# A two-block transformer forward pass on one core: the first pass over the experts as straight-line code, no token gather behind the last pair of experts, and the last expert's result leaving in two column halves

## What is computed

```
def moe_swiglu(u, w_router, w_gate, w_up, w_down):
    B, S, D = u.shape
    t = u.reshape(B * S, D)
    logits = (t @ w_router).astype(F32)
    top_vals, top_idx = lax.top_k(logits, TOP_K)
    top_w = jax.nn.softmax(top_vals, axis=-1)
    gates = jnp.sum(jax.nn.one_hot(top_idx, N_EXPERTS, dtype=F32) * top_w[..., None], axis=1)
    out = jnp.zeros((B * S, D), F32)
    for e in range(N_EXPERTS):
        y = swiglu(t, w_gate[e], w_up[e], w_down[e]).astype(F32)
        out = out + gates[:, e:e + 1] * y
    return out.reshape(B, S, D).astype(u.dtype)
```

## Time and profile before

| | |
|---|---|
| median of 3 runs | 1900.12 us (1899.29 to 1902.54) |
| the profiled execution's own time | 1900.97 us |
| its span, first to last instruction | 1899.1 us |
| time outside the span | 1.87 us |
| PE busy | 1819.6 us (96%) |
| DVE busy | 1482.6 us (78%) |
| ACT busy | 1246.3 us (66%) |
| POOL busy | 23.5 us (1%) |
| the chain that ended last | PE 85%, DVE 7%, ACT 6%, issue 2% |
| mean granted clock of PE | 0.979 |

### The profile page before, as it was taken

The page is one execution under the profiler, slowest core; times in us unless marked ns, Lnnn a source line. Parts: engine busy times, 40 slices in busy tenths (PEclk is TensorE's granted clock), DMA queues, the critical chain, the costliest instruction groups (busy, mean ns, idle before and its releaser), DMA issues.

```text
span 1899.1 us, 26739 instructions
## 1 busy us (share of the span) xinstructions
PE 1819.6 (96%) x9912; PEld 1560.7 (82%) x9912; DVE 1482.6 (78%) x1503; ACT 1246.3 (66%) x1288; POOL 23.5 (1%) x24
## 2 busy tenths in 40 slices
PE   7888999998999999999899999999999999999997
PEld 7777899887789988877788888888888888788886
DVE  7975788566567755665888988889878888798896
ACT  6966656365654435654677777777777777777776
POOL 0000000000000000000000000000000000000000
PEclk9999999999899999999899999999999999999999
DMA  9422455542235454434599999999999999999995
GB/s 373 150 89 89 156 179 186 193 175 89 89 120 190 180 185 160 165 111 152 200 384 358 394 374 338 379 364 392 373 331 373 367 396 373 331 366 377 378 371 190
DMA packets 69523, 495.69 MB, mean 261 GB/s; under 512 B 7840, under 2 KB 8224, under 8 KB 10144
## 3 DMA queue, kind: packets, MB, share of 16 engines
q1 hardware_dynamic: 67680, 487.48, 67.5%
q0 software_dynamic: 1728, 6.55, 1.6%
HBM read 488.76 MB, written 5.24 MB: 260 GB/s over the span
## 4 chain that ended last, share of the span: by engine, by line
PE 85%; DVE 7%; ACT 6%; issue 2%; DMA 0%; SPq 0%; POOL 0%; ACTq 0%; DVEq 0%; POOLq 0%
PE ps L424 26%; PE ps L426 20%; PE ps L433 20%; PE ps L435 6%; PE ps L428 6%; DVE wl L2130 2%; ACT wh L1401 2%; PE ps L1326 1%; PE ps L444 1%; PE ps L1247 1%; PE ps L839 1%; PE ps L840 1%; PE ps L844 1%; DVE hTl L2188 1%; ACT hTh L1439 0%
## 5 line engine op out<-in xcount | busy, mean ns | idle before, releaser
L3088 DVE TENSOR_TENSOR wl<-raw,wh 128x2048 fp32r<-128x2048 f32 x336 | 762.5, 2290 | 100.4 <-ACT wh L2038 99.5
L2038 ACT ACTIVATE wh<-raw 128x2048 fp32r<-128x2048 f32 x336 | 643.4, 1919 | 179.9 <-PE ps L433 179.9
L424 PE MATMUL ps<-wh,hTh 128*128 128x512 f32 (+2 forms) x1128 | 445.2, 396 | 9.5 <-issue 4.7
L426 PE MATMUL ps<-wh,hTl 128*128 128x512 f32 (+2 forms) x1128 | 436.5, 388 | 0.0
L2130 DVE TENSOR_TENSOR wl<-raw,wh 128x2048 fp32r<-128x2048 f32 x124 | 283.5, 2290 | 124.0 <-ACT wh L1401 123.8
L1401 ACT ACTIVATE wh<-raw 128x2048 fp32r<-128x2048 f32 x125 | 238.6, 1914 | 137.8 <-PE ps L433 70.2
L433 PE MATMUL ps<-wl,hTh 128*128 128x512 f32 (+2 forms) x1128 | 301.6, 387 | 0.0
L424 PEld LDWEIGHTS ps<-wh,hTh 128*128 128x128 f32 x1128 | 213.0, 189 | 54.2 <-issue 9.5
L424 PE MATMUL ps<-wh,work_r 128*128 128x512 f32 x648 | 255.7, 395 | 0.0
L426 PE MATMUL ps<-wh,work_r 128*128 128x512 f32 x648 | 253.0, 390 | 0.0
L426 PEld LDWEIGHTS ps<-wh,hTl 128*128 128x128 f32 x1128 | 213.3, 189 | 40.4
(11 more groups left out here) (432 smaller groups left out, 1539.3 us busy)
## 6 DMA issues: line engine op xcount, KB each, us to landing
raw<-in_units SPq DMA_DIRECT2D x461, 1024.0 KB, 7.0
x<-in_x SPq DMA_DIRECT2D x2, 512.0 KB, 5.3
work<-in_lru_w SPq DMA_DIRECT2D x1, 1024.0 KB, 15.0
xn<-in_mem SPq DMA_DIRECT2D x1, 1024.0 KB, 17.4
out<-x POOLq DMA_DIRECT2D x2, 512.0 KB, 6.9
consts<-in_consts POOLq DMA_DIRECT2D x1, 768.0 KB, 4.7
xn<-in_moe_gain POOLq DMA_DIRECT2D x1, 512.0 KB, 5.9
consts<-in_consts SPq DMA_DIRECT2D x1, 354.0 KB, 11.3
```

The lines of the kernel that those rows point to most:

```text
L424: nc.tensor.matmul(out, sh, mh, start=(first and j == 0), stop=False)
L426: nc.tensor.matmul(out, sl, mh, start=False, stop=False)
L2038: A(wh[:, n % SPLIT, :], raw[:, n % RAW, :], ACT.Copy).then_inc(sem("hi_made"), 1)
L3088: V.tensor_tensor(wl[:, n % SPLIT, :], raw[:, n % RAW, :], wh[:, n % SPLIT, :].bitcast(F32), ALU.subtract).then_inc(sem("lo_made"), 1)
```

## The change

PE, ACT and DVE get their first pass over the experts as straight-line code: a Python loop over eight experts in place of the hardware loop, with constants in place of the registers. The loop stays for the pass under the `If`. In the last expert of the first pass the gather, `choose`, the splitting of the gathered tokens and the preparation of three further units fall away; they stand at the beginning of the `If`'s body now, and SyncE's loads of the three units as well. The last two down units of the last expert are computed one output half after the other: half h=0 over both units, then half h=1 over both. ACT scales each half as it is done, and POOL issues one indirect DMA for each. For that, out is also seen as rows of 512 columns, and the slots' table carries three row numbers (the full row, and twice it and twice it plus one), so that a tiny matmul is four columns wide in place of two.

```
         def experts(first, last):
-            with nc.tensor.Fori(first // 2, last // 2) as p:
-                for i in range(2):
-                    expert(p, i)
+        def experts():
+            for e in range(NE):
+                expert(e // 2, e % 2, last=(e == NE - 1))
...
-            if i == 1:
+            if i == 1 and not last:
                 pe.wait_ge(sem("chosen"), p + 2)
                 pe.wait_ge(sem("bank7_free"), p * 6 + 6)
                 for q in range(4):
                     gather(q)
             pe.wait_ge(sem("expert_hid"), of(ECH, ECH))
+            if last:
+                w = {}
+                for h in range(2):
+                    hs = slice(h * HALF, (h + 1) * HALF)
+                    for half in range(2):
+                        if h == 0:
+                            w[half] = unit_of(("down", ECH - 1, half))
+                        ins = split_product(ps[:, 4 + h, :],
+                                            [(ehh[(ECH - 1) % 2][:, 2 * half + k, :], ehl[(ECH - 1) % 2][:, 2 * half + k, :],
+                                              w[half][0][:, k, hs], w[half][1][:, k, hs]) for k in range(2)],
+                                            first=False, last=(half == 1), rest=rest_of(("down", ECH - 1, half)))
+                        if h == 1:
+                            ins.then_inc(sem("unit_used"), 1)
+                        elif half == 1:
+                            ins.then_inc(sem("first_half"), 1)
+                return
...
             def hi(j):
+                if last and j >= E_UNITS:
+                    return
...
                     for h in range(2):
+                        if last and h == 0:
+                            act.wait_ge(sem("first_half"), 1)
+                        else:
+                            act.wait_ge(sem("unit_used"), of(E_UNITS, E_UNITS + SPLIT))
...
+        rows_turned(NE - 1, TT + NE - 1)
+        for h in range(2):
+            pool.wait_ge(sem("y_scaled"), 2 * NE + h + 1)
+            G_.indirect_dma_start(out_halves, bass.IndirectOffsetOnAxis(ap=out_row[:, 1 + h:2 + h], axis=0),
+                                  y[:, h * HALF:(h + 1) * HALF], None, compute_op=ALU.add).then_inc(sem("out_written"), 16)
+        pool.wait_ge(sem("out_written"), 16 * (TT + NE + 1))
```

More of the change, by code:

```diff
@@ L1249, in gather, with over_experts, expert @@
             ins.then_inc(sem("bank7_full"), 1)
-        def experts(first, last):
-            with nc.tensor.Fori(first // 2, last // 2) as p:
+        def experts():
+            for e in range(NE):
+                expert(e // 2, e % 2, last=(e == NE - 1))
+        def over_experts():
+            with nc.tensor.Fori(NE // 2, NE) as p:
                 for i in range(2):
                     expert(p, i)
-        def expert(p, i):
+        def expert(p, i, last=False):
             def of(m, n):
@@ L1333, in _ @@
             gather(q)
-        experts(0, NE)
+        experts()
         with nc.tensor.If(nc.tensor.value_load(over[0:1, 0:1], min_val=0, max_val=1)):
-            experts(NE, 2 * NE)
+            pe.wait_ge(sem("chosen"), NE // 2 + 1)
+            pe.wait_ge(sem("bank7_free"), NE // 2 * 6)
+            for q in range(4):
+                gather(q)
+            over_experts()
     @block.sync
@@ L1373, in follow @@
             load(None, n, units_d[source])
-        for j in range(SPLIT):
-            follow(N_UNITS + j, N_FIXED + j)
         sp_.wait_ge(sem("routed"), 1)
         with nc.sync.If(nc.sync.value_load(over[0:1, 0:1], min_val=0, max_val=1)):
+            for j in range(SPLIT):
+                follow(N_UNITS + j, N_FIXED + j)
             groups = (NE * E_UNITS - SPLIT) // RAW
@@ L2023, in tokens_high, with experts, over_experts, expert @@
               ACT.Copy).then_inc(sem("tokens_hi"), 1)
-        def experts(first, last):
-            with nc.scalar.Fori(first // 2, last // 2) as p:
+        def experts():
+            for e in range(NE):
+                expert(e // 2, e % 2, last=(e == NE - 1))
+        def over_experts():
+            with nc.scalar.Fori(NE // 2, NE) as p:
                 for i in range(2):
                     expert(p, i)
-        def expert(p, i):
+        def expert(p, i, last=False):
             def of(m, n):
@@ L2069, in _ @@
             tokens_high(q, q + 1)
-        experts(0, NE)
+        experts()
         with nc.scalar.If(nc.scalar.value_load(over[0:1, 0:1], min_val=0, max_val=1)):
-            experts(NE, 2 * NE)
+            for r in range(4):
+                tokens_high(r, NE // 2 * 6 + 1 + r)
+            for n in range(N_UNITS, N_UNITS + SPLIT):
+                act.wait_ge(raw_loaded[n % RAW], 16 * (n // RAW + 1))
+                act.wait_ge(sem("unit_used"), n - N_FIXED + 1)
+                A(wh[:, n % SPLIT, :], raw[:, n % RAW, :], ACT.Copy).then_inc(sem("hi_made"), 1)
+            over_experts()
     @block.gpsimd
@@ L3074, in _, with experts, over_experts, expert @@
             step(V.tensor_copy(gates[:, NE:2 * NE, t], gates[:, 0:NE, t]))
-        def experts(first, last):
-            with nc.vector.Fori(first // 2, last // 2) as p:
+        def experts():
+            for e in range(NE):
+                expert(e // 2, e % 2, last=(e == NE - 1))
+        def over_experts():
+            with nc.vector.Fori(NE // 2, NE) as p:
                 for i in range(2):
                     expert(p, i)
-        def expert(p, i):
+        def expert(p, i, last=False):
             def of(m, n):
@@ L3121, in expert @@
             lo(E_UNITS - 2 + SPLIT)
-        experts(0, NE)
+        experts()
         with nc.vector.If(nc.vector.value_load(over[0:1, 0:1], min_val=0, max_val=1)):
-            experts(NE, 2 * NE)
+            dve.wait_ge(sem("bank7_full"), NE // 2 * 6)
+            choose(NE)
+            for r in range(4):
+                tokens_low(r, NE // 2 * 4 + 1 + r)
+            for n in range(N_UNITS, N_UNITS + SPLIT - 1):
+                dve.wait_ge(sem("hi_made"), n + 1)
+                V.tensor_tensor(wl[:, n % SPLIT, :], raw[:, n % RAW, :], wh[:, n % SPLIT, :].bitcast(F32),
+                                ALU.subtract).then_inc(sem("lo_made"), 1)
+            over_experts()
     block_cm.__exit__(None, None, None)
```

50 lines of the change are left out of this document (26 added, 24 removed).

## The result

The changed kernel takes 1886.81 us (median of 5 runs, 1881.16 to 1888.92), the kernel before, in 5 runs with it, 1899.29 us (1896.59 to 1902.54). The ratio is 0.9928, 95% interval 0.9916 to 0.994, so it is faster by 0.7%, or 13.7 us by the ratio. Forecast were 1888.8 us and 12.1 us less than the profiled execution; that of the changed kernel took 1886.81 us, 14.2 us less. The median lies in the range of 1886.0 to 1893.5; before's median of these runs times the ratio, 1885.6 us, lies just under it.

What follows compares the result with a forecast made beforehand. PE's issue, its few stops and what follows its last matmul were taken as the bound. From 1900.97 us, 5.5 + 1.6 + 0.8 + 3.4 + 0.8 = 12.1 us go: 1888.9, stated as 1888.8 us; range 1886.0 to 1893.5.

Steps and rivals of the forecast that it cites:

- parts 1 to 4: Expert stage: PE's branch stalls go, 5.5 us; slow clock goes, 1.57; table-load delays go, 0.8; unrolled code costs nothing.
- Parts 1 to 3: Boundaries between expert pairs: PE's branch stalls 5.5 us, slow clock 1.6 us and table-load delays 0.8 us go.
- Part 3: First down unit of each pair: ACT's table load delays PE 0.26 us; three of four delays go, 0.8 us.
- Part 2, the slow clock: Behind the third boundary: PE's clock at 0.50 for 3.4 us; without the stall no fall, 1.57 us saved.
- Part 5, the tail: Last expert: PE ends 2.77 us earlier, scaling 3.40 us earlier in all, landing 0.8 us shorter.
- the new wait of 0.7 us: Last expert, half 0: PE waits for the last unit's wl, 0.74 us late, because half 0 covers both units first.
- The half pieces' landing: Second output DMA: 128 pieces of half length land 0.8 us sooner; bounds none to 1.75 us.
- POOL's 0.77 us from scaling to issue: Kernel's end: POOL issues each half's DMA 0.77 us behind its scaling, as in the kernel before.
- (a): Rival, expert stage: boundary stalls turn into other waits, only the tail's 4.2 us stay: 1896.8 us, chance 0.07.
- (c): Rival, expert stage: PE waits at each block of its new code, adding 48 us: 1937 us, chance 0.05.
- (d): Rival, expert stage: DMA becomes the bound, the 5.5 us return as waits for raw: 1894.4 us, chance 0.05.
- (b): Main case's upper side: clock falls once elsewhere, half pieces save nothing, last wait 1 us longer: 1892.2 us; no separate chance.

Runs made afterwards that it cites:

- PE's loop alone: Kernel before with ACT's and DVE's first pass written out, PE keeping its hardware loop: 1897.66 us, ratio 0.9996; second look 1895.47 us.
- the second half's DMA alone: Changed kernel without the first half's DMA, so the last expert's first 512 columns never reach the output: 1887.52 us, ratio 0.9931 to the kernel before.
- the unrolled kernel: Kernel before with its first pass written out on PE, ACT and DVE, old tail kept: 1892.96 us, ratio 0.997.

## Why the prediction was right and where it was wrong

**What bounds the kernel, parts 1 to 4:** right. The stall at a boundary is the turn of PE's own loop (PE's loop alone keeps it, PE unrolled loses it), and goes with the arrival of a packet of instructions; straight-line code runs without a wait for issue, and each boundary is now like the one of the earlier trace rows. Parts 1 to 3 together were 7.9 us and measured 8.10. Part 3 had the delay at the first down unit of each pair right in place and in sum, and it goes with ACT's and DVE's loops; but half of the 0.26 us needs PE's stall ahead of it, and that the table load makes it is argued from the order of the rows, not tested. It also said that the first expert's delay stays; it went: the stretch to the first mark is 0.47 us shorter, 0.12 of it with PE unrolled alone and all of it with ACT and DVE unrolled and PE looped. There the load of 1.28 us at the head of ACT's loop goes as well, which the prediction did not count; whether it is the cause was not tried.

**Part 2, the slow clock:** right in size (1.57 us) for the profiled execution. "Perhaps without the slow 3.4 us", the reason given for the lower median, was wrong: three executions of three have a slow stretch. A stall alone does not bring it; 2.47 us with only PE looped did not. What decides it stays open.

**Part 5, the tail:** PE's end was right within 0.02 us, the new wait of 0.7 us and its cause included. Two terms behind it were mis-sized. The half pieces' landing saves 1.60 us and not 0.8: it goes by the bytes, nearly at the bound of 1.75 that was given, as the second half's DMA alone shows at 4.83 us. And POOL's 0.77 us from scaling to issue was taken as fixed; behind another DMA it is 0.27 us, and 0.76 in all kernels where POOL had waited long.

**The failed step** is the term of the sum for the tail behind PE's last matmul: landing and way to the issue were put at 0.8 us and nothing, and measured 1.60 and some 0.5, so that the tail is 5.4 us and not 4.2. That is 1.2 of the 2.1 us by which the sum fell short; 0.7 are the two stretches ahead of the first mark, put at nothing, and 0.2 the boundaries. With the tail the range failed. Its lower end, 1886.0, let the landing save its whole 1.75 us, but took POOL's 0.77 us and the first expert's time as certain, and it left out how much the executions differ ahead of the expert stage, in code that the change does not touch: the first mark moves by 3.7 us between two traces of the changed kernel and by 5.6 us over all thirteen, and the five runs reach from 1881.16 to 1888.92 us. With the measured sizes the sum is 14.2 us, and 1900.97 - 14.2 = 1886.8.

The step from the profiled execution to the median was mis-sized too. The prediction names 0.85 us between them and takes 0.1 of it; all of it gives 1900.12 - 12.1 = 1888.0, and with the measured 14.2 us it gives 1885.9, just under the range. The low edge of its main case doesn't follow from its own terms either: 1888.8 - 0.95 - 0.85 is 1887.0 and not 1886.5. So the stages were forecast well, and the range was too narrow by terms that were taken as certain.

**The rivals.** (a), only the tail stays: falls with the unrolled kernel's 8.1 us in the stage. (c), a wait at each block of code: there is none, though blocks arrive: the instruction queue has 37 packets in the expert stage where it had 45, and 9 over the pair in which the prediction expected about 11. (d), the DMA as the bound: ACT has no wait for a load in the changed kernel either, at 122.01 us for each boundary. (b): none of its three terms came; the clock did not fall elsewhere, the half pieces saved 1.6 us, and the last wait was as long as forecast.

## What to carry to other kernels

Here each turn of a hardware loop with over 1,000 matmuls in its body cost the busiest engine 1.2 to 2.6 us (a short body was not tried). Look for the engine's waits for "issue" once per turn, compare with a place in the body where the same code runs straight on, and look in the instruction queue for a packet just ahead of the engine's new start. Writing the loop out on the busiest engine alone brought 7.8 of the 8.1 us. At a kernel's end, price each link behind the last matmul by itself (scaling, the way to the issue, landing, end), and once a result leaves in pieces look at the engine that issues them: here PE could end 0.9 us earlier and the kernel ended no earlier.

## What the runs showed that I had not expected

- The stall at PE's branch is not constant: 1.2 to 2.6 us in fifteen boundaries of five traces of looping kernels. What is nearly constant, 1.71 to 1.92 us, is the time from the end of a 16 KB packet of instructions to the next pair's first matmul.
- POOL issues an indirect DMA 0.76 us behind the end of the scaling it waited for when it had been waiting for long, and 0.27 us behind it when it had ended another issue 0.35 us before.
- An adding, scattered DMA of 128 pieces lands 4.8 to 5.1 us behind its issue with 2 KB pieces and 6.4 to 6.9 us with 4 KB pieces on otherwise quiet queues; two of them 1.87 us apart made the second one's landing 5.7 us.
- One slow stretch of PE's clock in the expert stage, 3.4 us at 0.50 (1.2 GHz), in each of three executions with all three engines looping, behind its longest stall, and none in two with PE's loop alone.
